# A hybrid decoder step on one core: the sampled sequences' states on strips of the array, without masked keys, and woven between the last value projections

## What is computed

```python
# HGRN, each of the 8 sampled sequences b and 8 heads h (S0 comes from memory, 64 KB a head):
o     = att @ v + (q * exp(G)) @ S0                    # 8 tokens, 128 wide
S_new = exp(g_last)[:, None] * S0 + (k * exp(g_last - G)).T @ v
# mLSTM, each sequence b and 4 heads h (C0 from memory, 256 KB a head):
num   = s @ v + w_inter[:, None] * (q @ C0)            # 8 tokens, 256 wide
C_new = decay * C0 + (w_state[:, None] * k).T @ v
# both new states go back to memory; 8 sequences x 2 branches x 2 layers
```

## Time and profile before

| | |
|---|---|
| median of 3 runs | 2506.62 us (2504.64 to 2511.58) |
| the profiled execution's own time | 2505.04 us |
| its span | 2503.3 us |
| PE busy | 2325.5 us (93%) |
| DVE busy | 1607.0 us (64%) |
| ACT busy | 1153.9 us (46%) |
| POOL busy | 119.6 us (5%) |
| mean granted TensorE clock | 0.961 of full |
| DMA, mean over the span | 188 GB/s |

### The profile page before, as it was taken

The page is one execution under the profiler, slowest core; times in us unless marked ns, Lnnn a source line. Parts: engine busy times, 40 slices in busy tenths (PEclk is TensorE's granted clock), DMA queues, the critical chain, the costliest instruction groups (busy, mean ns, idle before and its releaser), DMA issues.

```text
span 2503.3 us, 31442 instructions
## 1 busy us (share of the span) xinstructions
PE 2325.5 (93%) x13220; PEld 2036.5 (81%) x13220; DVE 1607.0 (64%) x1814; ACT 1153.9 (46%) x1154; POOL 119.6 (5%) x99
## 2 busy tenths in 40 slices
PE   7899999999889998889999899889999999999996
PEld 6788776789889997878866789778888888888884
DVE  5755645745554425755646655468988979889893
ACT  4443221234243325343221243356766767767673
POOL 1000022100000000000203000000000000000000
PEclk9999999999999998999889999989999999999998
DMA  5222342734434442223333634469988999989980
GB/s 163 68 89 94 97 141 71 230 117 152 152 101 154 141 128 81 72 89 106 117 96 114 214 103 150 169 227 329 363 327 324 367 324 368 330 321 365 330 325 22
DMA packets 312717, 471.14 MB, mean 188 GB/s; under 512 B 15082, under 2 KB 189434, under 8 KB 312568
## 3 DMA queue, kind: packets, MB, share of 16 engines
q1 hardware_dynamic: 312476, 469.04, 54.5%
q10 hardware_dynamic: 92, 0.00, 0.0%
HBM read 439.10 MB, written 29.92 MB: 187 GB/s over the span
## 4 chain that ended last, share of the span: by engine, by line
PE 49%; DVE 4%; ACT 2%; DMA 1%; issue 1%; DVEq 0%; SPq 0%; POOL 0%; ACTq 0%; POOLq 0%
PE bank L507 10%; PE bank L509 10%; PE bank L508 10%; PE bank L513 3%; PE bank L514 3%; PE bank L515 3%; PE bank L857 2%; PE bank L798 1%; PE bank L833 1%; PE bank L906 1%; PE bank L807 1%; DMA out_c_sample<-weights 1%; PE bank L675 1%; PE bank L665 1%; PE bank L702 0%
## 5 line engine op out<-in xcount | busy, mean ns | idle before, releaser
L1703 DVE TENSOR_TENSOR unit_rest<-weights,unit_high 128x2048 fp32r<-128x2048 f32 x198 | 452.1, 2289 | 85.2 <-ACT unit_high L1208 84.7
L1208 ACT ACTIVATE unit_high<-weights 128x2048 fp32r<-128x2048 f32 x198 | 379.3, 1919 | 159.0 <-PE bank L509 153.7
L1549 DVE TENSOR_TENSOR mixer_rest<-weights,mixer_high 128x2048 fp32r<-128x2048 f32 x96 | 219.6, 2289 | 240.0 <-ACT mixer_high L1085 240.0
L513 PE MATMUL bank<-tokens_in_high,mixer_high 128*128 128x320 f32 x896 | 286.3, 320 | 8.2 <-DVE tokens_in_rest L2186 6.4
L507 PE MATMUL bank<-unit_high,tokens_high 128*128 128x512 f32 (+1 forms) x768 | 290.7, 379 | 2.0 <-DVE tokens_rest L1709 2.0
L509 PE MATMUL bank<-unit_high,tokens_rest 128*128 128x512 f32 (+1 forms) x768 | 287.0, 374 | 0.0
L508 PE MATMUL bank<-unit_rest,tokens_high 128*128 128x512 f32 (+1 forms) x768 | 286.5, 373 | 0.0
L514 PE MATMUL bank<-tokens_in_rest,mixer_high 128*128 128x320 f32 x896 | 281.9, 315 | 0.0
L515 PE MATMUL bank<-tokens_in_high,mixer_rest 128*128 128x320 f32 x896 | 280.8, 313 | 0.0
L1085 ACT ACTIVATE mixer_high<-weights 128x2048 fp32r<-128x2048 f32 x96 | 183.0, 1907 | 113.4 <-PE bank L515 41.2
L513 PEld LDWEIGHTS bank<-tokens_in_high,mixer_high 128*128 128x128 f32 x896 | 174.0, 194 | 9.5 <-DVE tokens_in_rest L2186 6.9
(11 more groups left out here) (399 smaller groups left out, 4619.6 us busy)
## 6 DMA issues: line engine op xcount, KB each, us to landing
weights<-in_w_in SPq DMA_DIRECT2D x72, 1024.0 KB, 5.0
weights<-in_w_ex_gate SPq DMA_DIRECT2D x67, 1024.0 KB, 6.4
weights<-in_w_ex_up SPq DMA_DIRECT2D x66, 1024.0 KB, 6.3
weights<-in_w_ex_down SPq DMA_DIRECT2D x65, 1024.0 KB, 6.7
arena<-in_w_ex_down SPq DMA_DIRECT2D x23, 1024.0 KB, 6.7
arena<-in_w_ex_up SPq DMA_DIRECT2D x22, 1024.0 KB, 6.2
arena<-in_w_ex_gate SPq DMA_DIRECT2D x21, 1024.0 KB, 6.6
weights<-in_state_mlstm_c SPq DMA_DIRECT2D x16, 1024.0 KB, 6.0
```

The source lines that it names most:

```text
L513: nc.tensor.matmul(out, wh, xh, start=start, stop=False)
L1208: nc.scalar.activation(high[n % MOE_SPLIT], raw[n % MOE_RAW], ACT.Copy).then_inc(mo_high, 1)
L1549: nc.vector.tensor_tensor(wl, unit_at(l, *u)[0], wh, ALU.subtract).then_inc(*dv_s.done("unit rest", l, *u))
L1703: nc.vector.tensor_tensor(rest[n % MOE_SPLIT], raw[n % MOE_RAW], high[n % MOE_SPLIT], ALU.subtract)\
```

## The change

It does these things, in both layers:

- HGRN state output: the queries become the weights (`qzA`, 32 columns for a head and a sequence, of which 8 hold its tokens at their place and the others are zero), S0 moves (128 columns), and head h's output goes to the 32 PSUM partitions of strip g = h // 2. The sum over all 8 sequences for 8 heads fills one bank (`interA`), which ACT copies out (`interSA`), and 4 matmuls with the identity turn it into the outputs' bank (`hgrn_outputs`).
- State increments of both branches: no masked keys. Sequence b's 8 key rows and 8 value rows are copied to partitions 32 * (b % 4) on by small transfers (16 a branch and layer, 32 KB each, issued by ACT). The matmuls have 8 rows; two sequences alternate on two strips of rows and write two banks. The banks for them are four (pool "W": 3 to 6), for both branches.
- mLSTM output: the same with `qzB`, the four heads on the four strips of columns, one bank (`interB`) in place of two.
- POOL no longer masks keys; it clears and fills `qzA` and `qzB` (four of each a layer).
- Order: gates after two more fillers, then the four `bu` steps, then four times (the states of two sequences, three `bv` steps). In `MIXER` the S units alternate with the `bv` units. The `bv` weights' rounded parts (`LATE`) are made later, at ACT's fillers 15, 18, 22 and 26, and for the first and last in other homes. DVE: gate rows first, then four times (a quarter of the convolution, the states of two sequences, a `bv` rest).
- mLSTM's sampled states go in pairs of sequences: DVE updates two sequences, then normalises two HGRN heads.

The core of the diff:

```diff
+    out = [(n, i, part) for n, i in first[:-2] for part in range(2)]
+    for i in range(2):
+        for part in range(2):
+            out += [("S", 2 * i + part, 0), ("bv", i, part)]
+    out += [("C", i, 0) for i in range(DB)]
...
+LATE = [FIRST_HALF - 4 + i for i in range(4)]
+LATE_AT = (15, 18, 22, 26)
...
+        kA4 = view(a_x, 2, D)
+        vA4 = view(a_x + 2 * D, 2, D)
+        interSA = view(a_x + 4 * D, 512)
+        qzA = [view(a_x + 6 * H + i * D, 4 * 264) for i in range(2)]
...
+        pools = {n: Banks(b, holders) for n, b in (("G", [0, 1]), ("L", [2, 3, 4]), ("M", [5, 6]), ("S", [7]),
+                                                   ("I", [2]), ("W", [3, 4, 5, 6]))}
...
+            def hgrn_states(l, u):
+                if u == 0:
+                    claim(pe, "I", l, "interA")
+                    pe.wait_ge(*po_s.at("qzA", l))
+                inter = of(l, "interA")
+                w, full, n = unit_at(l, "S", u)
+                pe.wait_ge(full, n)
+                s0 = w.rearrange("p (b h v) -> p b h v", b=2, h=HA)
+                for e in range(2):
+                    b = 2 * u + e
+                    for hh in range(2):
+                        for g in range(4):
+                            h = 2 * g + hh
+                            mm = nc.tensor.matmul(inter[32 * g:32 * g + 32, chunk(2 * (b // 4) + hh)],
+                                                  qzA[b // 4][:, 256 * (b % 4) + 32 * h:256 * (b % 4) + 32 * h + 32],
+                                                  s0[:, e, h, :], start=b == 0 and hh == 0, stop=b == DB - 1,
+                                                  skip_group_check=True)
+                mm.then_inc(*pe_s.done("inter", l, u))
...
+                for q in range(2):
+                    outs = [claim(pe, "W", l, "dS", 2 * u + e, q) for e in range(2)]
+                    for j in range(4):
+                        for e in range(2):
+                            b, h = 2 * u + e, 4 * q + j
+                            g = slice(32 * (b % 4), 32 * (b % 4) + DS)
+                            mm = nc.tensor.matmul(outs[e][:, chunk(j)], kA4[g, b // 4, chunk(h)], vA4[g, b // 4, chunk(h)],
+                                                  start=True, stop=True)
+                    mm.then_inc(*pe_s.done("dS", l, u, q))
+            def hgrn_outputs(l):
 
...
+                pe.wait_ge(*ac_s.at("free", l, "interA"))
+                for i in range(4):
+                    mm = nc.tensor.matmul(oS[:, i % 2:HA:2, 32 * (i // 2):32 * (i // 2) + 32], interSA[:, chunk(i)], ident,
+                                          start=False, stop=True, skip_group_check=True)
+                mm.then_inc(*pe_s.done("oS", l))
...
+                inter = claim(pe, "I", l, "interB")
+                    if b % 4 == 0:
+                        pe.wait_ge(*po_s.at("qzB", l, b // 4))
+                    for c in range(2):
+                        for h in range(HB):
+                            o = 256 * (b % 4) + 32 * (2 * h + c)
+                            mm = nc.tensor.matmul(inter[32 * h:32 * h + 32, 256 * (b // 4):256 * (b // 4) + 256],
+                                                  qzB[b // 4][:, o:o + 32], c0[:, h, c, :], start=b == 0 and c == 0,
...
+                    if b % 2 == 1:
+                        for h in range(HB):
+                            outs = [claim(pe, "W", l, "dC", b - 1 + e, h) for e in range(2)]
+                            for c in range(2):
+                                for e in range(2):
+                                    r = b - 1 + e
+                                    g = slice(32 * (r % 4), 32 * (r % 4) + DS)
+                                    mm = nc.tensor.matmul(outs[e][:, c * 256:(c + 1) * 256],
+                                                          kB4[g, r // 4, h * 256 + c * P:h * 256 + (c + 1) * P],
+                                                          vB4[g, r // 4, h * 256:(h + 1) * 256], start=True, stop=True)
+                            mm.then_inc(*pe_s.done("dC", l, b // 2, h))
...
+                    if hf == 0:
+                        while todo:
+                            step()
+                step()
+                step()
+                gates(l)
+                for _ in range(4):
+                    step()
+                for u in range(DB // 2):
+                    hgrn_states(l, u)
+                    for _ in range(3):
                         step()
                 conv_rows(l)
+                hgrn_outputs(l)
...
+                if w == LATE[0]:
+                    act.wait_ge(*pe_s.at("st", l, 1))
+                    act.wait_ge(spread_rows["kA"], 16 * DB * (l + 1))
+                elif w % FIRST_HALF >= HOMES or w == FIRST_HALF or w == FIRST_HALF + 1:
...
+                act.wait_ge(*dv_s.at("qS", l, 1))
+                for b in range(DB):
+                    g = slice(32 * (b % 4), 32 * (b % 4) + DS)
+                    act.dma_start(kA4[g, b // 4, :], kTok[DS * b:DS * b + DS, 2, :]).then_inc(spread_rows["kA"], 16)
+                    act.dma_start(vA4[g, b // 4, :], vTok[DS * b:DS * b + DS, 2, :]).then_inc(spread_rows["vA"], 16)
+                act.wait_ge(load["gates"], 16 * (l + 1))
+                nc.scalar.activation(gwh, gw, ACT.Copy).then_inc(*ac_s.done("gates high", l))
+                step()
+                step()
...
+                unit_rest(l, LATE[0])
+                def hgrn_state(u):
+                    s0 = unit_at(l, "S", u)[0].rearrange("p (b h v) -> p b h v", b=2, h=HA)
+                    dve.wait_ge(*pe_s.at("inter", l, u))
                     for q in range(2):
+                        dve.wait_ge(*pe_s.at("dS", l, u, q))
+                        for e in range(2):
+                            b = 2 * u + e
...
+                    for e in range(2):
+                        table[("dve", "newS", l, 2 * u + e)] = dv_s.count
+                dve.wait_ge(*ac_s.at("free", l, "bu", 1, 3))
+                dve.wait_ge(*po_s.at("U", l))
+                dve.wait_ge(*pe_s.at("level", l, 1, 7, 0))
+                for j in range(CW):
...
+                    hgrn_state(j)
+                    if j < 3:
+                        unit_rest(l, LATE[j + 1])
+                    settle()
...
+                for p in range(DB // 2):
+                    dve.wait_ge(*pe_s.at("interB", l, 2 * p + 1))
                     for h in range(HB):
+                        dve.wait_ge(*pe_s.at("dC", l, p, h))
+                        for b in (2 * p, 2 * p + 1):
+                            c = unit_at(l, "C", b)[0].rearrange("p (h v) -> p h v", h=HB)[:, h, :]
+                            nc.vector.scalar_tensor_tensor(c, c, decB[:, h, b:b + 1], of(l, "dC", b, h), ALU.mult, ALU.add)\
+                                .then_inc(*free(dv_s, l, "dC", b, h))
+                            table[("dve", "newC", l, b)] = dv_s.count
+                    if p == 0:
                         dve.wait_ge(*ac_s.at("rsA", l))
                         dve.wait_ge(*ac_s.at("silu g", l))
...
+                    nc.gpsimd.memset(qzA[i][:, 0:D], 0.0).then_inc(*po_s.done())
+                pool.wait_ge(*dv_s.at("qS", l, 1))
+                for i in range(2):
+                    nc.gpsimd.tensor_copy(apart(qzA[i]), qS[:, :, 32 * i:32 * i + 32].rearrange("p h (b t) -> p b h t", b=4))\
+                        .then_inc(*po_s.done("qzA", l))
+                pool.wait_ge(*pe_s.at("nn", l, HB - 1))
+                pool.wait_ge(spread_rows["kB"], 16 * DB * (l + 1))
+                for i in range(2):
+                    nc.gpsimd.memset(qzB[i][:, 0:D], 0.0).then_inc(*po_s.done())
+                    pool.wait_ge(*po_s.last())
+                    nc.gpsimd.tensor_copy(apart(qzB[i]), qI[:, :, 32 * i:32 * i + 32].rearrange("p h (b t) -> p b h t", b=4))\
+                        .then_inc(*po_s.done("qzB", l, i))
```

More of the change, by code:

```diff
@@ L108, in mixer_units @@
     last = [(n, i) for n in ("pa", "ga", "bo", "gb", "pb", "wo") for i in range(2)]
-    out = [(n, i, part) for n, i in first for part in range(2)]
-    out += [("S", i, 0) for i in range(DB // 2)] + [("C", i, 0) for i in range(DB)]
+    out = [(n, i, part) for n, i in first[:-2] for part in range(2)]
[3 more added lines that the diff above has]
+    out += [("C", i, 0) for i in range(DB)]
     return out + [(n, i, part) for n, i in last for part in range(2)]
@@ L793, in sampled_mlstm @@
                     c0 = w.rearrange("p (h c v) -> p h c v", h=HB, c=2)
-                    pe.wait_ge(*po_s.at("qz", l, b))
-                    for h in range(HB):
-                        o = 256 * (h % 2)
-                        for c in range(2):
-                            mm = nc.tensor.matmul(inter[h // 2][0:NS, o:o + 256], qz[b % 2][:, 2 * h + c, :],
-                                                  c0[:, h, c, :], start=b == 0 and h % 2 == 0 and c == 0,
+                    if b % 4 == 0:
```

(26 more changed lines are left out.)

197 lines of the change are left out of this document (66 added, 131 removed).

## The result

The changed kernel takes 2494.31 us (median of 5, 2488.88 to 2495.45) against 2507.65 for the kernel before in the same session (5 runs): a ratio of 0.995, 95% interval 0.9937 to 0.9963. It is faster by 13 us where 41 were forecast, and 0.3 us outside the range. The profiled execution took 2495.11 us, its span is 2493.3, its mean granted clock 0.935 (0.961 before), and POOL's busy time fell from 119.6 to 31.1 us.

A forecast was written before the change was run, and what follows sets the result against it. PE, busy for 93% of the span, was taken as the bound, with DVE pacing mLSTM. Gains of 17.4 us (HGRN) and 2.5 (mLSTM) a layer, 39.8 over two, gave 2466 us; range 2446 to 2494.

The forecast's parts named there:

- the 16 small transfers: HGRN and mLSTM: ACT issue 0.3 us each, 4.8 us, hidden behind two `bu` pieces (7.1) or a waiting copy.
- SP's chain: SP's queue of stores and loads, eight rounds in mLSTM, moves no earlier; C5 and C7 late; mLSTM gain 2.5 us a layer.
- ready at 85 against 88 needed: End of mLSTM's stretch: the last `pa` unit is loaded and rounded at 85 us, before its need at 88.
- Two abreast: Strip outputs: only neighbouring matmuls' records overlap, whatever the number of strips; 1.9 us for a HGRN pair's output.
- two records on one strip: PE's in-order queue: both records of a matmul use one strip, so only one's second and the next's first share time.
- The 0.5 us for changes: HGRN states on PE: three changes a pair between strips and whole array cost 0.5 us, within 5.2 us a pair.
- the cover of 2 us a quarter: HGRN: DVE's 11.5 us a quarter against PE's 13.5; gone if PE's pair costs under 3.2, then DVE sets the pace.
- on time, or late by a few us in the bad case: HGRN loads behind S0's store (S2, third `bv` unit): ready 45 to 49 us after 240.90, needed by ACT at about 45.
- the 4 us of stalls: Sampled mLSTM: C5 and C7 arrive late, C7 near 47 us where DVE wants it at 43 to 45; 4 us put.
- the waits and the slow group of the earlier trace: HGRN: PE's 4.15 us wait for DVE's first update and the half-rate group behind it (3.75 us against 2.03) go.
- rival (a): Both stretches: strips run fully abreast, PE's pair 3.3 us, DVE bounds; HGRN 75.6, mLSTM 60.6, kernel 2451 us; chance 0.22.
- Rival (d): Both stretches: no change, `bv` units and C late by 15 us or so a layer; about 2500 to 2507; chance 0.07.

The follow-up runs named there:

- experiment 1: Changed kernel with SP instead of ACT issuing the 32 small transfers of a layer: 2475.51 us, ratio 0.9871.
- Experiment 7: Changed kernel with SP issuing the small transfers, and ACT instead of SP issuing the C stores: 2455.6 us, ratio 0.979.
- experiment 2: Changed kernel with only the loop order altered, so that matmuls of one strip stand next to each other: 2490.98 us, ratio 0.9937.
- experiment 5: Changed kernel with every small matmul on one strip, same count and shapes, outputs not the reference's: 2552.93 us in one run.
- Experiment 6: Changed kernel with SP issuing the small transfers, and DVE updating HGRN states ahead of the convolution's quarter: 2467.16 us, ratio 0.9835.
- the repairs: Changed kernel with SP issuing the row transfers, DVE updating HGRN states before the convolution's quarter, ACT issuing the C stores: 2447.81 us, ratio 0.9749.
- experiment 8: Changed kernel with SP issuing the small transfers, and extra unread matmuls keeping PE busy in the sampled mLSTM's waits: 2471.05 us, ratio 0.9853.
- 10: Changed kernel with all three repairs, and idle matmuls keeping PE busy in the sampled mLSTM's waits: 2447.47 us, ratio 0.9743.

## Why the prediction was wrong

- **The step that failed: the 16 small transfers.** "Issued at 0.3 us each as a like one (0.27), 4.8 us of ACT ... hidden. In mLSTM ... nothing." The row they were priced by is a load from memory; these, from one part of the on-chip memory to another, cost 0.66 each. With 10.7 us in ACT's way instead of 4.8, neither cover holds: 6.9 us in layer 0 at the gates (`qk_blocks` at 329.34, in experiment 1 at 321.26, head start off) and 4.3 at the head sums (a wait of 7.26 in place of 2.99), 11.2 in all. Experiment 1 gives back 19 us in the end. Forecast and result differ by 28; experiment 1's 2475.5 is 9.5 above the forecast.
- **The other 9.5: what SP's chain costs, mis-sized.** At the second head sums of layer 1 experiment 1 is 29.6 us ahead of the kernel before where 39.8 were forecast. HGRN's stretches give 34.6 (34.8 forecast), those from `qk_blocks` to `pa` lose 1.7 (5 to be gained), and the `pa` stretches lose 3.2, which the forecast left untouched ("ready at 85 against 88 needed"). Experiment 7, which only takes the C stores off SP, mends both.
- **The strips, mis-sized to the safe side.** Two abreast was wrong for the output: 1.0 us, not 1.9. Increments 2.0, at the lower bound. The reasoning from two records on one strip is refuted by experiments 2 and 5: outputs overlap even where the next matmul in the queue is on the same strip. The 0.5 us for changes was right. A pair costs 3.2 us with them, not 5.2, which is worth 8 us of PE a layer.
- **Why that was worth nothing:** the cover of 2 us a quarter was worked out for 5.2; the text had a point from which it is gone, 3.2 a pair, and this is at it (pairs 11.5 us apart, DVE's sum 11.5). In place of strip time PE waits for the third and fourth `bv` rests. So it is luck that experiment 1's HGRN stretch comes out as forecast (34.6 against 34.8): faster strips and unforeseen waits cancel. The third was called "on time, or late by a few us in the bad case"; it is 3.65 late, and 3.77 in experiment 1, where the gates are on time. Here DVE ended the first pair later than put (279.6 against 273.5), since the gates were late; and from S2's issue to the third unit in ACT's hands it took 9.7 us (8 put). Experiment 6: 8 us.
- **mLSTM's own stretch came near by luck (65.9 against 65).** Its parts were named rightly: DVE's pace, C5 and C7 late, some half-rate groups under DVE's cover. But the 4 us of stalls were 5.1 and 6.9, partly hidden, and where nothing holds the stretch up from outside (experiment 1) it takes 67.2 and 68.5 us, so it gains nothing. That this chain costs 20 us over both layers was not seen: SP's chain was taken as given. Experiment 7 shows it to be a matter of which queue issues the stores.
- **A reading of no weight:** one sequence's output took 1.71 us from start to start (315.65 to 317.36), not 1.85, which is the length of the record; the 3.6 for both is right.
- **What was right:** the waits and the slow group of the earlier trace rows go, POOL's and DVE's dropped work shows on no path (no run tests it alone), DVE's quarters and pairs cost what was summed, and rival (a)'s two numbers (75.6 and 60.6 us) are nearly what the kernel reaches with the repairs (78.0 and 60.5): 2447.8 against 2451, some of it from the `pa` stretch, which rival (a)'s sum does not have. Rival (d) was right in kind: SP's queue holds both stretches.
- **Open:** why both mixers' 14.0 us are only 10.0 at the end of the profiled pair. 2.7 of it is the router stretch at a lower clock; no run here changes that alone. Why the clock falls behind the state groups in experiment 2 and not in the change. And what strips, the order of the units and the dropped masks give apart from each other: experiment 5 prices the strips inside the changed kernel, but no run has the new order with the old matmuls.

## What to carry to other kernels

Small transfers are work of the engine that issues them: take their price from a row with the same kind of source and destination, and put them on a queue that nobody waits for. When a stage gets faster, list for each buffer who frees it, and walk the queue of stores and loads once with the new times; here one queue for both stores and loads cost 20 us, more than the 13 that the whole change gave. And price a part of a change with its faults mended before calling it worthless: the mLSTM part went from 5 us lost to 12 gained.

## What the runs showed of the hardware

- A small transfer within the on-chip memory (8 partitions, 32 KB) costs the issuing queue 0.66 us on ACT and 0.67 on SP, against 0.27 for a small load from memory.
- Strips overlap nearly as well with two matmuls of one strip in a row: output 1.12 us in place of 1.08, mLSTM's increments 2.10 in place of 2.00. With four in a row the increments take 2.82 in place of 2.05 (experiment 2).
- A pair of sequences has three changes of form: whole array, strips of columns, strips of rows, whole array. Each costs 0.1 to 0.2 us, 0.5 together: 3.57 us from 269.00 to 272.57, against 0.38 for the two whole-array records and 2.7 for the two groups at their inner pace (0.109 us for four output records, 0.112 for two increment records). A change between two whole-array forms shows no such cost (254.77 to 254.92 us in the kernel before, at a pace of 0.147). The Trainium skill (TensorEngine Tiling (Array Packing), Key Properties) says that a change of mode drains the engine; the trace agrees that it costs something, and shows how little.
- In the sampled mLSTM, where PE is busy for 40.4 of 65.9 us, the granted clock is 0.58 and a group of 16 increment records behind a wait takes 3.78 us in place of 2.00. Extra matmuls in the waits brought the rate back (1.07 us in place of 1.94 for an output) but did not shorten the stretch where a late C set the pace (69.9 us against 67.2, experiment 8), and gave nothing where DVE did (10).
- A busy PE can have a lower clock too: in experiment 2 it has no gap for 13.9 us, and the clock of that window is 0.88.
